# A float32 transformer stack on one core: the two places between a post-norm and the layer behind it, reordered on three engines

## The reference, cut to what matters

```
x = x + rms_norm(merged @ w_out[i], post_mix_norm[i])
h = rms_norm(x, pre_ffn_norm[i])
f = (jax.nn.silu(h @ ffn_w_gate[i]) * (h @ ffn_w_up[i])) @ ffn_w_down[i]
x = x + rms_norm(f, post_ffn_norm[i])
```

## Time and profile before

| | us |
|---|---|
| median of three runs | 1459.42 |
| the profiled execution's own time | 1459.41 |
| its span, first to last instruction | 1457.6 |
| TensorE busy with matmuls | 1366.9 (94% of the span), 12187 instructions |
| TensorE weight loads | 1308.1 (90%) |
| VectorE busy | 1036.4 (71%), 1709 instructions |
| ScalarE busy | 764.7 (52%), 1262 instructions |
| GpSimd busy | 110.6 (8%) |
| mean granted TensorE clock | 0.966 of full speed |

### The profile page before, as it was taken

The page is one execution under the profiler, slowest core; times in us unless marked ns, Lnnn a source line. Parts: engine busy times, 40 slices in busy tenths (PEclk is TensorE's granted clock), DMA queues, the critical chain, the costliest instruction groups (busy, mean ns, idle before and its releaser), DMA issues.

```text
span 1457.6 us, 29627 instructions
## 1 busy us (share of the span) xinstructions
PE 1366.9 (94%) x12187; PEld 1308.1 (90%) x12187; DVE 1036.4 (71%) x1709; ACT 764.7 (52%) x1262; POOL 110.6 (8%) x127
## 2 busy tenths in 40 slices
PE   7998999998798999997999799999999989999998
PEld 6997988896798999997998599999999988999986
DVE  5769899895686666557598977787565565788754
ACT  5584384335644544345467765444454546644543
POOL 2000000000100211000010100111000100011100
PEclk9999999898899999999999899999999999999999
DMA  8633510120154553763584335553766621455462
GB/s 265 179 106 126 174 58 2 61 89 31 58 189 130 173 174 116 246 192 116 158 234 146 102 118 172 178 196 93 248 185 173 203 87 59 145 181 194 160 210 79
DMA packets 199151, 211.55 MB, mean 145 GB/s; under 512 B 8634, under 2 KB 190666, under 8 KB 198874
## 3 DMA queue, kind: packets, MB, share of 16 engines
q1 hardware_dynamic: 196938, 201.39, 43.5%
q0 software_dynamic: 2000, 8.46, 2.0%
q10 hardware_dynamic: 96, 0.02, 0.0%
HBM read 208.22 MB, written 1.64 MB: 144 GB/s over the span
## 4 chain that ended last, share of the span: by engine, by line
PE 73%; DVE 15%; issue 5%; ACT 3%; DMA 2%; POOL 1%; SPq 0%; DVEq 0%; ACTq 0%; POOLq 0%
PE pb L434 19%; PE pb L436 18%; PE pb L435 18%; DVE w_lo L475 2%; DVE pj L1537 2%; PE pb L2571 1%; PE pb L2570 1%; PE pb L2569 1%; PE pb L2110 1%; DVE sub L1465 1%; PE pb L2496 1%; PE pb L2153 1%; PE pb L2099 1%; DVE sub L1466 1%; PE pb L2105 1%
## 5 line engine op out<-in xcount | busy, mean ns | idle before, releaser
L434 PE MATMUL pb<-x_hi,w_hi 128*128 128x256 f32 x1984 | 567.6, 286 | 19.6 <-DVE w_lo L475 9.9
L475 DVE TENSOR_TENSOR w_lo<-raw,w_hi 128x1024 fp32r<-128x1024 f32 (+2 forms) x384 | 469.3, 1225 | 153.2 <-ACT w_hi L469 152.3
L469 ACT ACTIVATE w_hi<-raw 128x1024 fp32r<-128x1024 f32 (+2 forms) x384 | 395.6, 1040 | 328.3 <-PE pb L436 262.2
L435 PE MATMUL pb<-x_lo,w_hi 128*128 128x256 f32 x1984 | 563.9, 284 | 0.0
L436 PE MATMUL pb<-x_hi,w_lo 128*128 128x256 f32 x1984 | 563.6, 284 | 0.0
L434 PEld LDWEIGHTS pb<-x_hi,w_hi 128*128 128x128 f32 x1984 | 383.5, 193 | 23.9 <-DVE w_lo L475 15.3
L435 PEld LDWEIGHTS pb<-x_lo,w_hi 128*128 128x128 f32 x1984 | 383.6, 193 | 0.2
L436 PEld LDWEIGHTS pb<-x_hi,w_lo 128*128 128x128 f32 x1984 | 383.4, 193 | 0.0
L706 POOL TENSOR_TENSOR sub<-sub,rstd 128x256 f32<-128x256 f32 x66 | 72.3, 1110 | 581.3 <-ACT sub L1034 581.3
L434 PE MATMUL pb<-act_hi,w_hi 128*128 128x256 f32 x392 | 111.9, 285 | 4.0 <-DVE w_lo L475 4.0
L436 PE MATMUL pb<-act_hi,w_lo 128*128 128x256 f32 x392 | 111.5, 284 | 0.0
(11 more groups left out here) (334 smaller groups left out, 2200.7 us busy)
## 6 DMA issues: line engine op xcount, KB each, us to landing
raw<-in_ffn_w_up_dram SPq DMA_DIRECT2D x55, 1024.0 KB, 5.1
raw<-in_w_in_dram SPq DMA_DIRECT2D x28, 1024.0 KB, 5.2
raw<-in_ssd_w_in_dram SPq DMA_DIRECT2D x20, 1024.0 KB, 5.4
raw<-in_ffn_w_down_dram SPq DMA_DIRECT2D x16, 1024.0 KB, 5.1
raw<-in_fox_w_in_dram SPq DMA_DIRECT2D x16, 1024.0 KB, 5.7
raw<-in_ffn_w_down_dram SPq DMA_DIRECT2D x16, 896.0 KB, 5.1
raw<-in_ffn_w_gate_dram SPq DMA_DIRECT2D x11, 1024.0 KB, 5.3
raw<-in_ssd_w_out_dram SPq DMA_DIRECT2D x8, 1024.0 KB, 5.4
```

The costliest lines, as they stand in the source:

```text
L434: pe.matmul(o, w_hi[m][:, k, :], hi[:, k0 + k, :], start=first and k == 0, stop=False)
L435: pe.matmul(o, w_hi[m][:, k, :], lo[:, k0 + k, :], start=False, stop=False)
L469: act.activation(piece(ly, w_hi[m], nk, m), raw_piece(ly, s, nk, m), ACT.Copy).then_inc(sem("w_hi_ready"), 1)
L475: dve.tensor_tensor(piece(ly, w_lo[m], nk, m), raw_piece(ly, s, nk, m), piece(ly, w_hi[m], nk, m).bitcast(F32), ALU.subtract).then_inc(sem ...
```

## The change

Six edits, all at the two places between a branch layer and its successor:

1. `BRANCH_ADDS` goes from 5 to 4. Tiles 1 to 4 are added by VectorE, the last of these additions now stands a block earlier, and TensorE sums tile 5 by itself: four calls of the ones matmul in place of three.
2. ScalarE's table load moves from behind the last block into the branch layer: into step 1 of `w_out`, and into the first step of unit 3 of `down0`.
3. VectorE's order in `post_norm` becomes scale 0, add 0, scale 1, add 1, low 0, scale 2, and from there scale `k+1`, add `k`, low `k-1`.
4. TensorE begins unit 0 with the eight products of `k` = 0 that need only `x_hi`, and waits for `x_lo` only before the four others.
5. In `up0` and `ssd_z` the weights of unit 1 are split one step earlier: block `m` of unit 1 at step `m` of unit 0, and so the first of them ahead of the root on ScalarE and ahead of the wait for the root on VectorE. The step (1, 0), which split block 3 before, splits nothing.
6. The bounds of the hooks that do the additions follow from edit 1.

```diff
-                        pe.matmul(o, w_hi[m][:, k, :], hi[:, k, :], start=k == 0, stop=False)
+                        pe.matmul(o, w_hi[m][:, k, :], hi[:, k, :], start=False, stop=False)
...
-                    for k in range(nk - 2):
+                    pe.wait_ge(sem("x_hi_ready"), in_base + 1)
+                    for m in range(done):
+                        pe.matmul(pb[m][:, 0:T], w_hi[m][:, 0, :], hi[:, 0, :], start=True, stop=False)
+                        pe.matmul(pb[m][:, 0:T], w_lo[m][:, 0, :], hi[:, 0, :], start=False, stop=False)
+                    pe.wait_ge(sem(in_ready), in_base + 1)
+                    for m in range(done):
+                        pe.matmul(pb[m][:, 0:T], w_hi[m][:, 0, :], lo[:, 0, :], start=False, stop=False)
+                    for k in range(1, nk - 2):
...
-        BRANCH_ADDS, TREE_ADDS, TILE_ADDS = 5, 2, 6
+        BRANCH_ADDS, TREE_ADDS, TILE_ADDS = 4, 2, 6
...
         def split_next(split, eng, ly, nxt, u, p, m, last):
-            if ly.name in SPREAD and isinstance(u, int) and u + m == 0:
-                return
+            if ly.name in SPREAD and isinstance(u, int):
+                if u == 0:
+                    split(eng, ly, 1, 1, m)
+                if u == 0 or (u, m) == (1, 0):
+                    return
...
             def post_norm(i, n, nxt):
 
-                log_exp()
                 act_head(act, nxt, 0, 0, M_PER_UNIT - 1)
...
             def w_out_hook(u, m):
                 j = M_PER_UNIT * u + m
+                if j == 1:
+                    log_exp()
...
             def down0_hook(u, m):
                 first = L["down0"].evac0
+                if (u, m) == (L["down0"].k_split, 0):
+                    log_exp()
...
-                scale(0)
-                for k in range(1, KC + 3):
-                    if k < KC:
-                        scale(k)
-                    if k < KC + 1:
-                        add(k - 1)
-                    if k >= 3:
-                        low(n, k - 3)
+                for k in range(2):
+                    scale(k)
+                    add(k)
+                low(n, 0)
+                scale(2)
+                for k in range(2, KC):
+                    if k + 1 < KC:
+                        scale(k + 1)
+                    add(k)
+                    low(n, k - 1)
+                low(n, KC - 1)
...
-                if j >= 3:
+                if 3 <= j < 3 + BRANCH_ADDS:
                     branch_add(0, j - 2)
...
-                if u == len(L["down0"]) - 1 and m >= 2:
-                    branch_add(1, M_PER_UNIT + m - 2)
+                if (u, m) == (len(L["down0"]) - 1, 2):
+                    branch_add(1, M_PER_UNIT)
...
                 pe.wait_ge(sem("sq_acc"), ACC_BRANCH[i])
                 mm(pb[7][:, 0:T], ones[:, :], sub[:, 0, :], start=True, stop=False)
-                pe.wait_ge(sem("osq_ready"), (KC - 1) * (i + 1))
-                mm(pb[7][:, 0:T], ones[:, :], sub[:, KC - 2, :], start=False, stop=False)
+                for k in (KC - 3, KC - 2):
+                    pe.wait_ge(sem("osq_ready"), (KC - 1) * i + k + 1)
+                    mm(pb[7][:, 0:T], ones[:, :], sub[:, k, :], start=False, stop=False)
```

## The result

The changed kernel took **1444.41 us** (median of 4 executions, 1442.38 to 1448.39) beside 1460.11 for the kernel before in the same session (1458.62 to 1460.94): ratio 0.9897, 95% interval 0.9874 to 0.992, so 1.0% faster. The forecast was 1449.8, range 1445.5 to 1454.0. Ten executions of the changed kernel, these four and six taken later, have a mean of 1445.1.

What follows compares the result with a forecast made beforehand. TensorE is busy for 94% of the span, so only its waits or lower clock can be won. 1.1 + 1.6 + 0.4 + 1.7 = 4.8 us a place, 9.6 in all: from 1459.41 to 1449.8 us, range 1445.5 to 1454.0.

Steps and rivals of the forecast that it cites:

- Edits 1 and 2: Norm's sums at each place: ones matmuls start before the last block is ready, so Ln comes 1.1 us earlier.
- The table load: ScalarE, in its new spot in the branch layer: its 1.28 us hide in a 1.45 us wait, so it loses nothing.
- Edits 3 and 4: From first scale to TensorE's first product of unit 0: 1.63 us in place of 3.21, so 1.6 us earlier.
- The price of the waits: VectorE's two adds right behind their scales: about 0.12 us extra each, counted in the sum.
- The new wait for `x_lo`: TensorE in unit 0, behind the first twelve products: up to 0.8 us of waiting for `x_lo` of `k` = 1.
- Edit 5: Ahead of unit 1: weights split earlier, so TensorE starts 0.2 us behind unit 0; 1.7 us gained a place.
- root and block 1: ScalarE's early split doesn't hold the root; unit 1's block 1 gets its weights with 1.1 us to spare.
- The clock in unit 0: One short slow stretch costing 1.6 us at each place; with the `x_lo` wait, unit 0 lasts 14.8 us, 0.4 gained.
- The clock doesn't fall: Rival for unit 0: clock stays up, a place gains 6.4 us, 1446.6 us in all; chance 0.17.
- later stages: Stages behind the places move by the sum; clock effect set at zero, 1.6 us more or fewer as bounds.

Runs made afterwards that it cites:

- `e2_sums`: Kernel before with only four VectorE additions, four calls of the ones matmul and the table load moved; 1454.8 us, ratio 0.9971.
- `e3_order_hi`: Kernel before with only VectorE's new order in `post_norm` and TensorE's eight early `x_hi` products; 1455.97 us, ratio 0.9978.
- `f4_three_early`: Changed kernel with the early product order for `k` = 0, 1 and 2, plus 10 idle ones matmuls at each place; 1441.24 us, ratio 0.9886.
- `f1_before_again`: Kernel before, unchanged, compared with itself; 1458.61 us, ratio 1.0003.
- `f2_no_split`: Changed kernel with the weights of unit 1 split as before, not one step earlier; 1454.88 us, ratio 0.996.
- `e7_after_low1_fill`: Changed kernel with low 1 directly behind scale 2 on VectorE and 10 idle ones matmuls behind the sums at each place; 1443.02 us, ratio 0.9887.
- `e6_after_low1`: Changed kernel with low 1 moved directly behind scale 2 on VectorE; 1444.92 us, ratio 0.9897.
- `e4_before_fill`: Kernel before with 17 idle 128-column ones matmuls into an unused bank behind the sums at each place; 1453.25 us, ratio 0.9962.

## Why the prediction was right in its sign and wrong in its size

**Edits 1 and 2** were right: 1.1 us, measured 1.14 (`e2_sums`). Ln came at 454.73, not near 455.3, but the whole first stage lay 0.52 us earlier in that trace (the square at 453.46 for 453.98): against the square it is 1.27 for the forecast 1.32. The table load cost nothing that shows.

**Edits 3 and 4** were right: 1.6 us, measured 1.59 (`e3_order_hi`), and both together 2.73 for 2.7. The price of the waits was in it: in the chain above the add starts 0.52 us behind its scale (455.69, 456.21). The Trainium skill (VectorE: DVE Perf Modes, "The DRAIN you can't avoid") has a semaphore cost nothing extra between two operations; here two scales that don't wait on each other start 0.40 us apart, and `e3_order_hi` gained what the sum with the 0.12 us in it gave.

**The new wait for `x_lo`** was right in place, and a little high in size: up to 0.8 us forecast, 0.48 of idle time in the row; with the slow start of the next product `f4_three_early` got back 0.62.

**Edit 5** was right at its wait (1.7, measured 1.65 or 1.66), and root and block 1 weren't held. What I missed stands behind it: I took from one trace that the clock stays at 1.00 after the 1.79 us ahead of unit 1. Over all traces it fell there at 6 places of 12, both of them in `f1_before_again` and in `f2_no_split`. Where it does, the edit is worth 3.0 us a place and not 1.7 (D and E of `f2_no_split`).

**The clock in unit 0** is the step that failed. I took the wait at 1023 us as the nearest row, and so one short slow stretch at each place: gained 0.4 us. At three of the four places seen in the changed kernel the clock didn't fall, and B went from 12.86 to 10.88: gained 2.0. That is 1.6 us a place and 3.2 in all, of the 5.0 by which the gain of the ten executions exceeds the forecast's 9.6. The rival *The clock doesn't fall* had 6.4 us a place, and D fell by 6.3 to 6.6, by which of the profiles are compared. It had 0.17, and was the right case; the time that it gave, 1446.6, is 1.5 us above the mean of the ten executions of the changed kernel (1445.1), and inside the range. The median of the four that the forecast met, 1444.41, lies 0.7 below that mean, so part of the miss of the range is the draw. The second place of the first profile (B 12.06) is the forecast's own case, and that execution, at 1448.39, lies 1.4 us from the forecast. The Trainium skill (TensorE: Matmul & The Clock Gate, "HAM oscillation") warns only of longer gaps than 2.6 us. By it the clock stays up; these traces agree at three places and disagree at the fourth, and at both of `e3_order_hi`, where the same 2.62 us stood with another gap close by.

Why my nearest row misled me: a length of idleness doesn't fix what the clock does. Behind the wait that I took, the clock fell in all ten traces in which it lasts 1.95 to 2.57 us; behind the longer 2.62 us ahead of unit 0 it fell at three places of ten. Another wait, of 2.08 us and 779 to 796 us from the start, was followed by a fall in seven traces of fourteen. Two of the three falls behind 2.62 us are those of `e3_order_hi`. `f2_no_split` has the same wait and stayed up at both places; it differs by edits 1, 2 and 6, and edit 1 makes the ones matmuls follow the products with nothing between. That edits 1 and 3 decide the clock together, though I costed them apart, is thus possible and not shown: were the three falls spread by chance over the ten places, both places of `e3_order_hi` would be among them once in 15 times. The rival is the moment at which a wait begins, which differs between executions of one kernel as their clocks do.

**The range** was too narrow for a second reason. Three executions of the kernel before within 2.2 us made the spread look small. Over 71 executions, those of the first comparison and of the experiments' sessions, it runs from 1452.26 to 1469.62, mean 1459.7. The first square of these traces lies anywhere between 449.4 and 455.2 us, in kernels that don't differ there or hardly. I had set later stages to 1.6 us either way and earlier ones to nothing.

**What stays open.** D gives 6.6 us and E 6.2 in the second profile of the changed kernel, 12.8 in all; the timed gain is 14.6 (1459.7 less 1445.1). The intervals of the ratios, 11.7 to 18.4 us in the first series and 10.1 to 17.7 in the second, hold both numbers. Which stage gives the other 2 us, if any, isn't settled. The stretch ahead of the places doesn't show it: the first square lies at 452.1 us on the mean of the five traces without edits 1 and 2, at 452.5 in the nine with them. Nor is it settled what makes the clock fall at one of two places with the same waits: no run sets the moment at which a wait begins. And the idle calls do something far behind them: the wait for weights near 1007 to 1023 us lasts 1.20 to 1.43 us in the four kernels that have them and the clock stays up, against 1.95 to 2.57 us and a fall in the ten others. That fits most of the lower E of `e7_after_low1_fill` and `f4_three_early` (789.0, against 792.0 in `e6_after_low1`). Why it is shorter isn't known.

## What to carry to other kernels

Price a wait of TensorE by its length and by the clock behind it, and take the clock from more than one execution: the same kernel with the same waits had B at 12.86 and at 11.54. A sum of single edits misleads likewise. The three groups of edits shortened D by 1.7, 2.5 and 0.9 us alone, 5.1 in sum, and by 6.5 together; but the 0.9 holds a fall of the clock at 588 us, and A, B and C alone give 6.7 in sum and 6.4 together. Where TensorE must stand idle, a row of cheap products in the gap (0.23 us each here) tells in one run how much of a place is clock, and may be left in. Before giving a range, look at how far a stage that nobody touches moves between executions.

## What the runs showed of the hardware

- A clock loss can be passed on. In the two profiles of the kernel before, the slow stretch in unit 0 differed by 1.3 us at the first place, and the shorter one was followed by another behind the 1.79 us wait; D was 205.0 and 204.8. It isn't always so: at the first place of `e2_sums` (B 11.64) and of `e4_before_fill` (B 10.16) no fall followed behind the same wait, and D was 202.5 and 202.3.
- TensorE's granted clock fell behind waits of 1.79, 2.08 and 2.62 us, and stayed at 1.00 behind other waits of the same three lengths: 6 falls of 12, 7 of 14 and 3 of 10.
- Seventeen float32 calls of the ones matmul with 128 columns took 3.96 us, 0.23 each, and delayed nothing (first product 0.42 us behind the last of them, waiting for `x_lo`).
